# Level-0 inverse by block transposition on VectorE, and the low parts of the weights in four operations: a two-block transformer kernel

## What is computed

```python
def rwkv7_scan(r, w, k, v, a, b):          # per head, state [64, 64]
    def step(state, inp):
        r_t, w_t, k_t, v_t, a_t, b_t = inp
        sa = jnp.einsum('bhvk,bhk->bhv', state, a_t)
        state = (state * w_t[:, :, None, :] + sa[..., None] * b_t[:, :, None, :]
                 + v_t[..., None] * k_t[:, :, None, :])
        return state, jnp.einsum('bhvk,bhk->bhv', state, r_t)
...
def hybrid_layer(x, ...):
    h = rmsnorm(x, norm_mix_pre)
    proj = h @ w_in                        # q, k, v, r/k/v of the recurrence, gates
    ...
    y_rw = rwkv7_time_mix(rw, ...) @ w_o_rw
    mixed = jax.nn.sigmoid(gate_a) * y_att + jax.nn.sigmoid(gate_b) * y_rw
    x = x + rmsnorm(mixed @ w_out, norm_mix_post)
```

## Time and profile before

| | |
|---|---|
| median of 3 runs | 4056.68 us |
| profiled execution | 4055.24 us, span 4053.5 us |
| TensorE busy | 3873.0 us (96%), granted clock 0.975 of full speed on the mean |
| VectorE busy | 1954.3 us (48%) |
| ScalarE busy | 1635.8 us (40%) |
| GpSimd busy | 1652.3 us (41%) |
| bytes moved | 379.52 MB, 94 GB/s on the mean |

### The profile page before, as it was taken

The page is one execution under the profiler, slowest core; times in us unless marked ns, Lnnn a source line. Parts: engine busy times, 40 slices in busy tenths (PEclk is TensorE's granted clock), DMA queues, the critical chain, the costliest instruction groups (busy, mean ns, idle before and its releaser), DMA issues. The chain is left out here.

```text
span 4053.5 us, 67108 instructions
## 1 busy us (share of the span) xinstructions
PE 3873.0 (96%) x28244; PEld 3167.8 (78%) x28244; DVE 1954.3 (48%) x3042; ACT 1635.8 (40%) x2723; POOL 1652.3 (41%) x902
## 2 busy tenths in 40 slices
PE   8999989999999899998899999989999999999998
PEld 6888867878887788886787888777878887787887
DVE  7777673246534777767324654436231123523112
ACT  5554444343334555444434333446233224523222
POOL 4444412434445444441243444534444444444443
PEclk9999999989999899999998999989999999999999
DMA  3111113325532211111332554221222322122332
GB/s 134 48 49 44 67 45 112 104 99 188 186 131 98 85 48 49 44 68 44 111 99 97 193 183 135 99 73 43 98 89 99 98 90 79 53 94 89 99 99 83
DMA packets 108731, 379.52 MB, mean 94 GB/s; under 512 B 12561, under 2 KB 12945, under 8 KB 107793
## 3 DMA queue, kind: packets, MB, share of 16 engines
q1 hardware_dynamic: 98208, 357.27, 25.9%
q10 hardware_dynamic: 10224, 17.97, 1.2%
HBM read 359.46 MB, written 15.73 MB: 93 GB/s over the span
## 5 line engine op out<-in xcount | busy, mean ns | idle before, releaser
L293 POOL TENSOR_TENSOR Wlo<-raw,Whi 128x1024 fp32r<-128x1024 f32 x552 | 1334.4, 2420 | 1995.2 <-ACT Whi L280 1995.0
L228 PE MATMUL ps<-hh,Whi 128*128 128x512 f32 x2864 | 1152.1, 402 | 27.9 <-DVE hl L377 10.1
L228 PE MATMUL ps<-hl,Whi 128*128 128x512 f32 x2864 | 1123.4, 392 | 0.0
L228 PE MATMUL ps<-hh,Wlo 128*128 128x512 f32 x2864 | 1123.2, 392 | 0.0
L280 ACT ACTIVATE Whi<-raw 128x1024 fp32r<-128x1024 f32 x552 | 581.8, 1055 | 708.9 <-PE ps L228 607.9
L228 PEld LDWEIGHTS ps<-hh,Whi 128*128 128x128 f32 x2864 | 542.7, 189 | 160.2 <-issue 28.3
L228 PEld LDWEIGHTS ps<-hl,Whi 128*128 128x128 f32 x2864 | 543.1, 190 | 116.7 <-issue 8.6
L228 PEld LDWEIGHTS ps<-hh,Wlo 128*128 128x128 f32 x2864 | 542.2, 189 | 115.8
L228 PE MATMUL ps<-gh,Whi 128*128 128x512 f32 x864 | 337.6, 391 | 3.8 <-POOL Wlo L293 3.8
L228 PE MATMUL ps<-gh,Wlo 128*128 128x512 f32 x864 | 336.2, 389 | 0.0
L228 PE MATMUL ps<-gl,Whi 128*128 128x512 f32 x864 | 336.1, 389 | 0.0
(11 more groups left out here) (363 smaller groups left out, 5913.6 us busy)
## 6 DMA issues: line engine op xcount, KB each, us to landing
raw<-in_stream SPq DMA_DIRECT2D x554, 512.0 KB, 3.5
ada<-in_ada SPq DMA_DIRECT2D x96, 512.0 KB, 4.6
park_x<-xT SPq DMA_DIRECT2D x2, 2048.0 KB, 7.3
park_yh<-yh ACTq DMA_DIRECT2D x16, 256.0 KB, 2.1
park_yl<-yl ACTq DMA_DIRECT2D x16, 256.0 KB, 2.3
xT<-park_x SPq DMA_DIRECT2D x2, 2048.0 KB, 8.8
yrh<-park_yh ACTq DMA_DIRECT2D x16, 256.0 KB, 8.0
yrl<-park_yl ACTq DMA_DIRECT2D x16, 256.0 KB, 7.9
```

The source lines that it names most:

```text
L228: last = pe.matmul(ps, left[a](k), right[c](k), start=start and k == 0 and i == 0, stop=stop and k == n - 1 and i == 2)
L293: pool.tensor_tensor(b["Wlo"][:, slot], b["raw"][:, raw_slot(b, u)], b["Whi"][:, slot].bitcast(F32), SUB) \
```

## The change

First, each low part becomes four operations of 256 columns, of which the last raises the semaphore. Second, at level 0 VectorE makes also Wc = TM + I on all 128 partitions, without changing halves, and transposes it into X in blocks of 32 x 32 (of a 64 x 64 block of level 0 only the two diagonal blocks of 32 x 32 hold anything). TensorE's 16 matmuls and ScalarE's two copies per pair go. GpSimd's TM of level 2 and TensorE's W of level 1 now wait for VectorE. The mixing of `r` stays ahead of level 0, and that of `k` behind it.

```diff
@@ -36,6 +36,7 @@
 LEAD = 2
 PART = 8
 GRING = 12
+LOW_PIECES = 4
 ADA, ADA_LAG, SUM_LAG = 2, 3, 4
 ADA_W, ADA_K = 512, 2
 ADA_N = KD // ADA_K
@@ -290,8 +291,10 @@
     for u in range(max(first, LEAD), end):
         pool.wait_ge(s["w_hi"], u - LEAD + 1)
         slot = weight_slot(b, u)
-        pool.tensor_tensor(b["Wlo"][:, slot], b["raw"][:, raw_slot(b, u)], b["Whi"][:, slot].bitcast(F32), SUB) \
-            .then_inc(s["w_lo"], 1)
+        for i in range(LOW_PIECES):
+            part = slice(i * UNIT // LOW_PIECES, (i + 1) * UNIT // LOW_PIECES)
+            last = pool.tensor_tensor(b["Wlo"][:, slot, part], b["raw"][:, raw_slot(b, u), part], b["Whi"][:, slot, part].bitcast(F32), SUB)
+        last.then_inc(s["w_lo"], 1)
 
 
 def stream_loads(sp, s, b, first, end, beside=None):
@@ -447,11 +450,11 @@
 FRONT_A = Steps("trA", "trB", "trK", "trV")
 FRONT_V = Steps(*[f"T{i}" for i in range(8)])
 INV_G = Steps("m00", "m01", *[f"m{l}{h}" for l in range(1, LEVELS) for h in range(2)])
-INV_P = Steps("X00", "X01", *[f"{m}{l}{h}" for l in range(1, LEVELS) for m, h in
+INV_P = Steps(*[f"{m}{l}{h}" for l in range(1, LEVELS) for m, h in
                               (("W", 0), ("W", 1), ("X", 0), ("T", 0), ("X", 1), ("T", 1))
                               if not (m == "X" and l == LEVELS - 1)])
-INV_A = Steps("d00", "d01", "d10", "d11", "X00", "X01", *[f"W{l}{h}" for l in range(1, LEVELS) for h in range(2)])
-INV_V = Steps("t00", "T00", "t01", "T01", *[f"{m}{l}{h}" for l in range(1, LEVELS) for h in range(2) for m in "XT"
+INV_A = Steps("d00", "d01", "d10", "d11", *[f"W{l}{h}" for l in range(1, LEVELS) for h in range(2)])
+INV_V = Steps("t00", "T00", "i0", "t01", "T01", "i1", "X00", "X01", *[f"{m}{l}{h}" for l in range(1, LEVELS) for h in range(2) for m in "XT"
                               if not (m == "X" and l == LEVELS - 1)])
 TAIL_P = Steps("GV", "U0", "U1", "Z0", "Z1", "L0", "L1", "M", "N", "RY0", "RY1", "S2", "S3", "Y")
 TAIL_A = Steps("GV", "U0", "U1", "Z0", "Z1", "L0", "L1", "N0", "N1")
@@ -719,20 +722,10 @@
     def into(u, bank, c, left, right):
         return pe.matmul(b["ps"][half(u), bank, block(c)], left[:, block(c)], right[:, block(c)], start=True, stop=True)
 
-    for h in range(2):
-        pe.wait_ge(s["inv_v"], INV_V(p, f"T0{h}"))
-        for c in range(BLK):
-            for u in range(2):
-                last = pe.matmul(b["ps"][half(1 - u), 4 + h, block(c)], b["XT"][half(u), h, block(c)], b["c"]("identc")[half(u)],
-                                 start=True, stop=True)
-        last.then_inc(s["inv_p"], 1)
     for l in range(1, LEVELS):
         for h in range(2):
             pe.wait_ge(s["inv_g"], INV_G(p, f"m{l}{h}"))
-            if l > 1:
-                pe.wait_ge(s["inv_v"], INV_V(p, f"X{l - 1}{h}"))
-            else:
-                pe.wait_ge(s["inv_a"], INV_A(p, f"X0{h}"))
+            pe.wait_ge(s["inv_v"], INV_V(p, f"X{l - 1}{h}"))
             for c in range(BLK):
                 for u in range(2):
                     last = into(u, 2 + h, c, b["TM"][half(1 - u), h, l % 2], b["X"][half(1 - u), h])
@@ -912,9 +905,6 @@
 
 
 def rwkv_inv_act(act, s, b, p, between):
-    for h in range(2):
-        act.wait_ge(s["inv_p"], INV_P(p, f"X0{h}"))
-        act.activation(b["X"][:, h], b["ps"][:, 4 + h, 0:BLK * CB], ACT.Copy).then_inc(s["inv_a"], 1)
     for l in range(1, LEVELS):
         for h in range(2):
             act.wait_ge(s["inv_p"], INV_P(p, f"W{l}{h}"))
@@ -1103,7 +1093,7 @@
                 pool.wait_ge(s["inv_a"], INV_A(p, f"d{h}1"))
             else:
                 if l >= 2:
-                    pool.wait_ge(s["inv_p"], INV_P(p, f"W{l - 2}{h}") if l > 2 else INV_P(p, f"X0{h}"))
+                    pool.wait_ge(*((s["inv_p"], INV_P(p, f"W{l - 2}{h}")) if l > 2 else (s["inv_v"], INV_V(p, f"X0{h}"))))
             pool.tensor_tensor(blocks(b["TM"][:, h, l % 2]), blocks(b["TD"][:, h]), lvl[:, l].broadcast_to([P, BLK, CB]), MUL)                 .then_inc(s["inv_g"], 1)
         between(l)
 
@@ -1115,6 +1105,10 @@
         for u in range(2):
             dve.tensor_tensor(blocks(b["XT"][half(u), h]), blocks(b["TM"][half(1 - u), h, 0]), ident[half(1 - u)], ADD) \
                 .then_inc(s["inv_v"], 1)
+        dve.tensor_tensor(blocks(b["Wc"][:, h]), blocks(b["TM"][:, h, 0]), ident, ADD).then_inc(s["inv_v"], 1)
+    for h in range(2):
+        dve.wait_ge(s["inv_v"], INV_V(p, f"i{h}"))
+        dve.transpose(b["X"][:, h], b["Wc"][:, h]).then_inc(s["inv_v"], 1)
     between(0)
     for l in range(1, LEVELS):
         for h in range(2):
```

## The result

The change made the kernel slightly slower: 4064.28 us median of 20 runs (4059.19 to 4067.73) against 4058.38 (4051.76 to 4060.91) for the kernel before, a ratio of 1.0017 with a 95% interval of 1.0011 to 1.0024. The prediction was 4039, with 4054 as its upper end. The profiled execution took 4066.27 us, its span is 4064.5. So about 5 of the 11 us that the traces have to explain are scatter between executions of one kernel.

What follows compares the result with a forecast made beforehand. TensorE, busy 3873.0 of 4053.5 us, was taken as the bound. Savings of 17.5, 0.8 and 3.6 us less a cost of 4.4 gave -17.5: 4037.7 from the profiled 4055.2, 4039 as a median, range 4033 to 4054.

Steps and rivals of the forecast that it cites:

- what leaves TensorE: Level 0 of each pair: 16 matmuls go, so the first W starts 1.25 us earlier if X is ready.
- the walk: VectorE's operations timed through one pair, with GpSimd turns of 0.4 us: X of level 0 has 1 us of cover.
- the prediction's sum: Whole kernel: 17.5 and 0.8 saved in the pairs, 3.6 at the starts, 4.4 lost to low parts: -17.5 us.
- the cost of the low parts: Where TensorE waits for low parts: 8 waits 0.4 us longer, two of them 0.6 more, 4.4 us in all.
- the last pairs: Last pair of each layer: less cover for X of level 0, so a gain of about 0.4 us, twice.
- the start: Start of each layer's recurrence: TensorE's waits for `v` and `TB` go, 1.9 + 1.7 = 3.6 us.
- the walk of VectorE's backlog: After X of level 0: five to eight GpSimd turns, X of level 1 at 206.3, kkr at about 209.7.
- the thinnest place: ScalarE's chain behind kkr, up to the copy of zp: ends at 213.4, due at 213.7, cover 0.3 us.
- The signs of being wrong: TensorE waiting at L720 for X or Wc, a transposition over 0.7 us, VectorE waiting through more than one piece.
- the turns behind level 1: VectorE after X of level 1: cm, cum and kkr follow, kkr at about 209.7 against 209.35 before.
- The first rival: Chain kkr, exponentials, zp, Wc of level 3: backlog 1.1 us longer hands back 0.8 us per pair, 4050; chance 0.24.
- The third rival: VectorE/GpSimd ports change hands only after whole operations: turns cost 0.7 us, X of level 1 late, 4063; chance 0.08.

Runs made afterwards that it cites:

- e2: The changed kernel with low parts whole again, so only VectorE's transposition against the kernel before: 4088.05 us, ratio 1.0083.
- e10: The changed kernel with low parts in four only beside the recurrence and each pair's second low part behind TM of level 4: 4035.29 us, ratio 0.9951.
- e11: The kernel before, without the transposition, plus e10's two GpSimd edits: 4054.9 us, ratio 0.9997.
- e3: The changed kernel with TensorE's mean moved behind the half product of r at level 2: 4049.02 us, ratio 0.9978.
- e5: e3 with low parts in four only beside the recurrence and whole everywhere else: 4043.67 us, ratio 0.9966.
- e1: The kernel before with only the low parts in four, no transposition: 4059.61 us, ratio 1.0006.
- e7: e5 with each pair's second low part behind TM of level 4 instead of level 3: 4038.36 us, ratio 0.9953.

## Why the prediction was wrong

**Right: what leaves TensorE.** The pairs save 1.25 us each, and X is there in time. The first W had 1 us of cover in the walk; in pair 2 the second X ended at 199.47, TensorE's first W began at 200.02. The price of the transposition was taken as 0.42 us and is 0.414. A turn with GpSimd was taken as 0.4 and costs 0.43 (Wc 0.860 on the mean; in e2 one stood alone and took 0.43). e10 against e11 agrees with the size: 19.6 measured, 14 x 1.25 + 2 x 0.4 = 18.3 forecast. And e10, without the backlog and without pieces outside the recurrences, is 21.0 us below the kernel before (20 by the ratio), where the prediction's sum without the cost of the low parts is 18.3 + 3.6 = 21.9. One slip stands in the walk: behind the first two sums of XT it names "three more and the two Wc"; there are two more, and its 4 x 0.46 has them right.

**Right: the last pairs and the start.** The last pair of a layer waits 1.05 us for X of level 0 where 0.85 was reckoned. The waits for `v` and `TB` are gone. By the twin matmuls each layer's start saves 1.95 us; 1.8 was forecast.

**The step that failed: the walk of VectorE's backlog stopped at kkr.** The prediction took kkr as the last thing on VectorE that anyone waits for, and ScalarE's chain as "the thinnest place". The next instruction, the bonus product `rk`, was not looked at. TensorE's mean uses the PSUM bank that it reads, and so waits for it (`claim`). Its cover of 1.05 us before the change was thinner than the 1.25 by which TensorE was to move up. In pairs 1 to 6 of the kernel before the dependence left no trace in the list of waits, since it was covered; its only row there is that of the last pairs, 0.8 us twice. The signs of being wrong had TensorE waiting at L720 for X or Wc, and not here. Even the prediction's own figure for kkr, 209.7, gives it away: `rk` would end at 209.7 + 0.6 = 210.3, and the mean is wanted at 211.00 - 1.25 = 209.75. That is 0.55 us of stall in each of 12 pairs, 6.6 us, from its own numbers.

**Mis-sized: the turns behind level 1.** The rest of the 1.5 us is backlog. The walk counted five to six turns ahead of X of level 1, and that was right: the scans end 6.02 us after GV, and the walk had 5.7 to 6.6. But it counted none behind it, where `fe` took 0.70 instead of 0.16 and `cum` 1.19 instead of 0.69, 1.0 us together, beside the two TM of level 4 (206.85 to 208.28). kkr ends 10.28 after GV; the walk had 9.53. The first rival named this backlog, at 0.8 us per pair, and TensorE's chain behind kkr as its outlet. That outlet exists (e3: 0.5 us per pair), but the bonus product, 1.5 us, came first and hid it. So the rival was the right kind of case with too small a size: the pairs handed back all that they had won, 12 x 1.54 and, in pair 0 of the two layers, 1.80 and 1.74, together 22.0 us against 17.5.

**Nearly right: the low parts.** The cost of the pieces outside the recurrences was put at 4.4 us, 8 waits by 0.4 and two by 0.6 more. Waits grew by 5.0 us (11.8 to 16.8), which is near, in 10 places instead of 8. By the twin matmuls of the two profiled executions the stretches outside the recurrences lost 9.8 us; what the sum lacked is the longer time at the lower clock, of which the fall at 657 is 1.4 us, and part of it is scatter. The medians even that out: e5 against e3 gives 5 us for the pieces there, and e1 gives 6.4 (2.5 above the kernel before, although its starts save 3.9). So this term was short by 0.6 to 2 us and is not what failed. The small steps at the other places were not traced one by one.

**The third rival did not happen.** Turns cost 0.43, not 0.7, and X of level 1 was there 6.3 us after GV (205.28), where that rival had 9.1 (209.3). So it is not what made the kernel slow; that the time is close to its 4063 is chance. (The 4063 is 8 above the profiled 4055.2; from the median, as the other cases are given, it would be 4065.) The Trainium skill (SBUF — State Buffer, section "SBUF: two separate sides") has the other side blocked for the whole instruction; here Wc lost 0.43 us beside GpSimd operations of 0.77 on the mean, less than their recorded duration. Behind a whole low part of 2.4 us one Wc took 2.52 (e2), which agrees with the rule that the holder is not interrupted.

As a sum: 4055.2 less 17.5 (the matmuls) less 3.9 (the starts), plus 22.0 handed back in the pairs, plus 9.8 outside the recurrences, is 4065.6; the profiled execution took 4066.3. With the medians, 4058.4 before and 5 to 6.4 outside the recurrences, it is 4064.0 to 4065.4; 4064.3 was measured.

## What to carry to other kernels

When the bound engine moves up by some time, list everything that it takes from the other engines behind that point, with its cover before the change, also what hardly shows as a wait or not at all: a dependence with less cover than the gain takes the gain. Walk the late engine to the end of its backlog, not to the first instruction that is known to matter. And where an edit frees one engine from waiting for the bound one, ask what it will now run beside: here GpSimd, no longer held back by TensorE, fell on the scans, and moving one of its operations by one level was worth as much as the edits on TensorE and ScalarE together (4035.3 and 4037.4 us, the same within what these runs tell).

## What the runs showed of the hardware that was not expected

- VectorE's transposition of 32 x 32 blocks of fp32 takes 414 ns for 128x256, the mean of 32 of them, the same as a sum of that size with one operand in PSUM (0.41).
- An operation of GpSimd cut in four costs more than its parts: Wlo of 128x1024 takes 2.41 us (the mean of e5's 472 whole ones). The four of 128x256 that replace it are recorded at 0.768 each on the mean and overlap in the records; GpSimd was busy with the 2208 of them for 1625.7 us, 2.95 for each unit. Some took turns with VectorE; four took 2.83 us where VectorE was mostly idle (e7, 208.76). So the cut by itself costs some 0.4 us, as forecast, and the turns the rest.
- In the first layer a wait of 3.63 us instead of 2.76 was followed by a stretch at the lower of TensorE's two levels. In windows of 1 us of the changed kernel (columns as above), TensorE waits until 657.24, runs at full clock (2.4 GHz), at 0.50 (1.2 GHz) from about 658.6 to 662, and then at full clock again, though it has been busy without a gap since the wait:

```profile
657.00:658.00 1.00, 0.76 (x3) 0.67 (x4) 0.00 (x0) 0.68 (x2) 0.91 (x3) 1.00 1.07 391
...
659.00:660.00 1.00, 1.00 (x4) 0.81 (x3) 0.00 (x0) 0.00 (x0) 1.00 (x2) 0.50 1.04 397
...
662.00:663.00 1.00, 1.00 (x6) 0.83 (x5) 0.00 (x0) 0.00 (x0) 0.00 (x0) 1.00 0.85 344
```

No run tried what makes the clock fall. At this place it fell behind the wait of 3.63 us, and not behind that of 2.76 in the kernel before or of 2.83 in e5. At the twin place in the second layer it fell in all three: behind 3.72 us in the changed kernel, 3.04 in the kernel before, and at the end of one of 2.83 in e5. So the length of the wait alone does not tell.
